# Meta token products over both weight blocks at once, key rows padded to 128, and output transposes moved up in TensorE's order

## The chip, the cores and the metric

The kernel runs on one NeuronCore of a Trainium2 chip. The metric is the device time of one execution in microseconds; the median of three runs before the change is 1068.54 us (1067.28 to 1068.82). The engines named are TensorE (PE, its weight loads PEld), VectorE (DVE), ScalarE (ACT), GpSimd (POOL) and SyncE (SP, which only issues loads).

## The reference, cut to what matters

A decoder block over 1024 tokens of width 1024, with 16 learned meta tokens put in front. Everything starts from one normalised input `h` and a wide product.

```python
z = jnp.concatenate([meta, x], axis=1)                  # 16 + 1024 tokens
h = rms_norm(z, norm_w[l])
p = (h @ w_in[l] + b_in[l]).astype(f32)                 # 1024 x 8192 weights
q, fz, iv, g_hg, u, g_pool, m_hg, m_pool = jnp.split(p, split_at, axis=-1)
log_f = jnp.log(lb + (1.0 - lb) * jax.nn.sigmoid(fz))   # forget gates, 8 heads of 128
k = (1.0 - lb) * jax.nn.sigmoid(-fz)                    # keys
o = hgrn2_chunkwise(q, k, iv, log_f)                    # S = diag(f) S + k v^T, o = S^T q
o = rms_norm(o, hg_norm_w)                              # per head
y_hg = (o * jax.nn.silu(g_hg)) @ w_down_hg[l]
pooled = causal_multiscale_pool(u)                      # windows 2, 4, 8, 16
y_pool = (mixed * pool_scale[l] * jax.nn.silu(g_pool)) @ w_down_pool[l]
merged = jax.nn.sigmoid(m_hg) * y_hg + jax.nn.sigmoid(m_pool) * y_pool
z = z + merged @ w_out[l]
return rms_norm(z, final_norm_w)[:, N_META:]            # meta tokens dropped
```

The meta tokens matter to the output only through what looks back at them: the gates, keys and values of the heads (F and V), and the pooled input (U).

## The kernel before, in words

**Pairs and products.** The weights are cut into blocks of 128 output columns, and two blocks make a pair; there are 40 pairs. `PAIRS` names them: FV (forget gate and value of a head), QG (its query, and the output gate of the head before), and so on; pair 16, in the last turn (j = 8) of the head loop, is an MM pair that has no meta tokens. A pair is computed by a scheme with seven products (`PRODUCTS`) instead of eight, with sums of the four half blocks as weights. Each product has 4 steps of k, and each step 3 matmuls of 128x512: operands are split into a high part (`w_hi`, `r_hi`) and a rest (`w_lo`, `r_lo`), and `three` (line 1149) multiplies high by high, high by rest and rest by high. `half(p, i, part)` issues one half of product i, six matmuls.

**What feeds a product.** For each product ScalarE makes `w_hi` (line 680), VectorE `w_lo` (line 1515), three products ahead of TensorE. ScalarE moves results out of the accumulators (`copy_first`, `last_quarter`), VectorE adds them (`add_11`, ...). All engines run lists written out by hand, and semaphores tie them together; nothing reorders them.

**Meta tokens.** For the 12 pairs FV and U the 16 meta rows are computed apart, in fp32. `meta_product` uses `hm` (the meta tokens, transposed, 16 of 32 columns filled) as stationary operand and the raw weight blocks as moving one: for each block, both halves of k and four column groups of the array, which write to four groups of rows in `acc[3]`. ScalarE copies that to `mt`, and `meta_turn` adds the four groups and turns the result with a small matmul against `stack`; ScalarE places it (`meta_place`). Raw blocks lie in three slots of a ring, block b in slot b % 3.

**A head.** The loop over j = 1 to 8 does the products of pairs FV(j) and QG(j) (14 products, counter n), and puts between them the work of head r = j - 1: `step` (levels of the within-chunk attention, line 1286), `v_transposes`, `k_transposes`, `k_times_v` (for each chunk keys times values; the meta tokens' product is one matmul with 16 rows, line 1305), `outputs` (line 1319, 1320). The normalised output of the head before, `vv`, is turned by `o_transposes(r - 1)` (line 1326), eight transposes, in the middle of product n = 3.

**The way to `o_normed`.** Outputs of head r - 1 are squared on ScalarE (`square_o`); in the next turn VectorE does `ahead(p, 0)`, `mean_o` (line 1768), the operations of `level(r, 0)`, `ahead(p, 1)`, then `normalise_o` (line 1776, two multiplications), which posts `o_normed`; GpSimd takes the power -1/2 in between (line 593). Behind the transposes VectorE's `gated_o` multiplies them with the gate.

Of the kernel before, what the change touches and what calls it, by code (L numbers as in the profile page):

```python
# [6 lines left out]
ACT = mybir.ActivationFunctionType  # L7
AX = mybir.AxisListType
F32 = mybir.dt.float32
# [3 lines left out]
P = 128  # L13
D = 1024
NK = D // P
SEQ = 1024
META = 16
L = META + SEQ
HEADS = 8
CHUNKS = SEQ // P  # L20
LEVELS = 7
STEPS = 6
HALF = 512
KH = NK // 2
# [25 lines left out]
RAWS = 3  # L50
# [62 lines left out]
GROUP = 32  # L113
# [6 lines left out]
def fv(j):  # L120
    return 2 * j

def qg(j):
    return 2 * j + 1
# [30 lines left out]
def hybrid_block(nc, x, meta, norm_w, wstream, pool_w, b_in, lb_logits, hg_norm_w, pool_scale, final_norm_w, out):  # L156
    names = ExitStack()
    with names:
# [4 lines left out]
            "masks_spread", "near_spread", "pool_step", "vec_step", "act_step", "bias_made", "lb_made",  # L163
            "x_squared", "x_mean", "x_rstd", "h_row", "h_tr", "h_hi", "h_copied", "h_lo", "v5_made", "v5_hi",
            "v5_lo", "v6_made", "v6_hi", "v6_lo", "v7_made", "v7_hi", "v7_lo", "v4_made", "v4_hi", "v4_lo",
            "hm_cleared", "hm_copied",
            "sums_made", "w_hi", "w_lo", "wo_hi", "wo_lo", "mm_done", "copied", "added", "c21_done", "meta_mm", "mt_copied", "mt_turned", "meta_placed",
            "qt_made", "prepared", "v_tr", "v_copied", "level_mm", "level_done", "k_tr", "k_copied", "kv_mm",
            "state_done", "o_mm", "o_squared", "o_mean", "o_rstd", "o_normed", "o_tr", "a_made", "a_stored0", "a_stored1",
# [10 lines left out]
        S = {n: names.enter_context(nc.semaphore(n)) for n in sem_names}  # L180
# [4 lines left out]
        def at(name, shape, dtype, offset=None):  # L185
            size = 4 if dtype != U8 else 1
            for n in shape[1:]:
                size *= n
            if offset is None:
                offset = here[0]  # L190
                here[0] += (size + 31) // 32 * 32
            assert offset + size <= 229368, (name, offset + size)
            return nc.alloc_sbuf_tensor_at(name, shape, dtype, offset=offset)
# [24 lines left out]
        w_hi = [at(f"w_hi{n}", [P, KH * P], F32R, ring_at + n * 4096) for n in range(RING)]  # L218
        w_lo = [at(f"w_lo{n}", [P, KH * P], F32R, ring_at + n * 4096 + 2048) for n in range(RING)]
        here[0] = ring_at + RING * 4096  # L220
        raw = [at(f"raw{n}", [P, D], F32) for n in range(RAWS)]
        sums_at = here[0]
        sums = [at(f"sum{n}", [P, HALF], F32) for n in range(4)]
        snaps_at = here[0]
# [6 lines left out]
        hm = at("hm", [P, 2, KH, GROUP], F32)  # L231
# [11 lines left out]
        gt = at("gt", [P, SEQ], F32)  # L243
        gs = at("gs", [P, HALF], F32)
        vv = at("vv", [P, SEQ], F32)
        vm = at("vm", [META, P], F32)
        km = at("km", [META, P], F32)
        st_at = here[0]
        st = at("st", [P, SEQ], F32)
        prod = at("prod", [P, HALF], F32)  # L250
# [5 lines left out]
        mt = at("mt", [P, 2 * P], F32, work + 52736)  # L256
        stack = at("stack", [P, META], F32, work + 53760)
# [65 lines left out]
        acc = [names.enter_context(nc.psum_tensor(f"acc{n}", [P, HALF], F32)) for n in range(4)]  # L323
        levels = names.enter_context(nc.psum_tensor("levels", [P, 2, HALF], F32))
        lev, small = levels[:, 0, :], levels[:, 1, :]
        miscs = names.enter_context(nc.psum_tensor("miscs", [P, 2, HALF], F32))
        misc = (miscs[:, 0, :], miscs[:, 1, :])
        VM, KM, KVM = slice(128, 256), slice(256, 384), slice(384, 512)
# [11 lines left out]
        raw_loaded = (S["raw_loaded0"], S["raw_loaded1"], S["raw_loaded2"])  # L340
# [60 lines left out]
        def turned(p, n):  # L401

            bank = misc[0] if p == 0 else acc[(p + 1) % 2]
            return bank[:, n * META:(n + 1) * META]

        def bias_of(p, n):
            mat, blk = PAIRS[p][1 + n]
# [2 lines left out]
        def raw_half(p, n, half):  # L410
            return raw[(2 * p + n) % RAWS][:, half * HALF:(half + 1) * HALF]
# [8 lines left out]
        def raw_count(p, n):  # L420
            return 16 * ((2 * p + n) // RAWS + 1)
# [115 lines left out]
        def _(pool):  # L537
# [47 lines left out]
            for g in range(GROUPS):  # L585
                rows = slice(g * GROUP, (g + 1) * GROUP)
                pool.tensor_copy(mask[rows, 0, :], whole[rows, rows])
                ins = pool.tensor_copy(mask[rows, 2:MASKS, 0:16], mask1[rows, 2:MASKS, g * 16:(g + 1) * 16])
            ins.then_inc(S["masks_spread"], 1)

            def o_rstd(r):
                pool.wait_ge(S["o_mean"], r + 1)
# [42 lines left out]
            for u in range(16):  # L635
                x = u % 4
                n, t = QUARTERS[x]
# [28 lines left out]
        def _(act):  # L666
# [243 lines left out]

            def copy_v(r):
                act.wait_ge(S["v_tr"], r + 1)
                for q in range(2):
                    act.activation(vv[:, q * HALF:(q + 1) * HALF], misc[q][:, :], ACT.Copy)
                act.activation(vm[:, :], small[0:META, VM], ACT.Copy).then_inc(S["v_copied"], 1)

            def spread_near(r):

# [8 lines left out]
            def copy_k(r):  # L927
                act.wait_ge(S["k_tr"], r + 1)
                for q in range(2):
                    act.activation(ek[:, q * HALF:(q + 1) * HALF], misc[q][:, :], ACT.Copy)  # L930
                act.activation(km[:, :], small[0:META, KM], ACT.Copy).then_inc(S["k_copied"], 1)

            def square_o(r):
                act.wait_ge(S["o_mm"], r + 1)
# [71 lines left out]
            for j in range(1, HEADS + 1):  # L1006
                p, q, r = fv(j), qg(j), j - 1
# [121 lines left out]
            for v in range(2 * CHUNKS):  # L1129
# [3 lines left out]
                if v >= CHUNKS:  # L1133
                    n, t = v - CHUNKS, T_ORDER[v - CHUNKS]
# [9 lines left out]
        def _(pe):  # L1144
# [25 lines left out]
            def meta_turn(p):  # L1170

                pe.wait_ge(S["mt_copied"], META_AT[p] + 1)
                if p:
                    pe.wait_ge(S["c21_done"], p)
                for n in range(2):
                    ins = pe.matmul(turned(p, n), mt[:, n * P:(n + 1) * P], stack[:, :], start=True, stop=True)
                ins.then_inc(S["mt_turned"], 1)

            def meta_product(p):

                if p:
                    pe.wait_ge(S["added"], ADDED[p - 1, 12])
                else:
                    pe.wait_ge(S["hm_copied"], 1)
                for n in range(2):
                    pe.wait_ge(raw_loaded[(2 * p + n) % RAWS], raw_count(p, n))
                    for h in range(2):
                        for k in range(KH):
                            ins = pe.matmul(acc[3][k * GROUP:(k + 1) * GROUP, n * P:(n + 1) * P], hm[:, h, k, :],  # L1190
                                            raw_half(p, n, h)[:, k * P:(k + 1) * P], start=h == 0, stop=h == 1)
                ins.then_inc(S["meta_mm"], 1)

            def half(p, i, part):
# [72 lines left out]
            def step(r, i):  # L1267
                m = STEP_LEVEL[i]
                if m:
                    pe.wait_ge(S["level_done"], r * STEPS + i)  # L1270
                else:
                    pe.wait_ge(S["prepared"], r + 1)
                for c in range(CHUNKS):
                    if m <= 4:
                        for g in range(GROUPS):
                            t = slice(c * P + g * GROUP, c * P + (g + 1) * GROUP)
                            if m == 0:
                                q = ek[:, t]
                            elif m == 1:
                                q = qx[:, :, t].rearrange("p a (b h j) -> p a b h j", h=2, j=2)[:, :, :, 1, :]  # L1280
                            elif m == 2:
                                q = qq[:, c, :].rearrange("p (n t) -> p n t", n=3)[:, :, g * 16:(g + 1) * 16]
                            else:
                                q = qt[:, t.start + 16:t.stop]
                            n = NEAR[m]
                            ins = pe.matmul(lev[g * GROUP:(g + 1) * GROUP, c * n:(c + 1) * n],
                                            kt[:, META + t.start:META + t.stop], q, start=True, stop=True)
                        continue
                    n = 1 << m
                    for h in range(64 // n):  # L1290
                        k0, row = c * P + h * 2 * n, h * 64 + c % 2 * n
                        ins = pe.matmul(lev[row:row + n, c // 2 * n:(c // 2 + 1) * n],
                                        kt[:, META + k0:META + k0 + n], qt[:, k0 + n:k0 + 2 * n], start=True, stop=True)
                ins.then_inc(S["level_mm"], 1)
# [28 lines left out]
            def o_transposes(r):  # L1323
                pe.wait_ge(S["o_normed"], r + 1)
                for c in range(CHUNKS):
                    ins = pe.transpose(misc[c // 4][:, (c % 4) * P:(c % 4 + 1) * P], vv[:, c * P:(c + 1) * P],
                                       ident[:, :])
                ins.then_inc(S["o_tr"], 1)
# [34 lines left out]
            for j in range(1, HEADS + 1):  # L1363
                r = j - 1
                for n in range(2 * PRODUCTS):
                    p, i = fv(j) + n // PRODUCTS, n % PRODUCTS
                    if n == 2:
                        step(r, 1)
                    elif n == 8:
                        step(r, 3)  # L1370
                    elif n == 9:
                        step(r, 4)
                    elif n == 10:
                        step(r, 5)
                    elif n == 11:
                        k_transposes(r)
                    elif n == 12:
                        k_times_v(r)
                    elif n == 13:
                        outputs(r)  # L1380
                    elif n == 5:
                        v_transposes(r)
                    elif n == 6:
                        step(r, 2)
                    half(p, i, 0)
                    if n == 0:
                        step(r, 0)
                    elif n == 3 and r:
                        o_transposes(r - 1)
                    half(p, i, 1)  # L1390

            for p in range(P_POOL, N_PAIRS):
# [8 lines left out]
            for v in range(2 * CHUNKS):  # L1401
                n, t = v // CHUNKS, T_ORDER[v % CHUNKS]
# [894 lines left out]
```

## Time and profile before

| | |
|---|---|
| median of 3 runs | 1068.54 us |
| profiled execution | 1068.12 us |
| its span, first to last instruction | 1066.4 us |
| TensorE matmul, weight load | busy 97%, 79% |
| VectorE, ScalarE, GpSimd | busy 73%, 46%, 9% |
| DMA | mean 98 GB/s |
| mean granted TensorE clock | 0.996 |

The three 128x512 groups of line 1149 alone take 445.7, 434.1 and 433.6 us of busy time, which overlap, since a matmul begins before the one before it is through. For the time that a row costs, the distance to the next row's start is what counts. An fp32 matmul shows as two records. In the profile's timeline an entry of several records runs from the first one's start to the last one's end. A mark in brackets at the end of an entry is the engine's idle time before it and what ended it.

### The profile page before, as it was taken

How to read it: one execution, taken by the hardware profiler on the slowest of the kernel's cores; microseconds unless marked ns; L12 is line 12 of the kernel's file. 1: busy time of each engine (PE TensorE's matmuls, PEld its weight loads, DVE VectorE, ACT ScalarE, POOL GpSimd, SP SyncE). 2: the span in 40 equal slices, each digit the busy share in tenths (PEclk: the TensorE clock that was granted, in tenths of full speed). 3: DMA queues.
4: the chain of work that ended last, by engine and by line, in shares of the span. 5: the costliest groups of instructions: out<-in, count | busy, mean ns of one | idle time of the engine just before them, and what ended most of it. 6: DMA issues, size and time to landing. Idle time of an engine off the chain costs nothing. (4 is left out here: it accounts for less than half of the span.)

```text
span 1066.4 us, 18850 instructions
## 1 busy us (share of the span) xinstructions
PE 1030.7 (97%) x7444; PEld 842.1 (79%) x7444; DVE 781.4 (73%) x1269; ACT 490.0 (46%) x829; POOL 98.0 (9%) x164
## 2 busy tenths in 40 slices
PE   7889999999999999999999999999999999999995
PEld 6668888888888888878888888788887786887884
DVE  7888787878787878787566877864479689878133
ACT  7663535454545453544353433434456345345122
POOL 2500010101010101010101010011100110001111
PEclk9999999999999999999999999999999999999998
DMA  7022020202020202021312222237322764545232
GB/s 261 1 79 80 22 81 21 81 21 81 21 81 21 80 21 80 25 95 53 99 41 89 60 89 79 70 119 266 128 80 98 283 230 158 190 166 178 70 127 100
DMA packets 36055, 104.61 MB, mean 98 GB/s; under 512 B 4576, under 2 KB 4576, under 8 KB 35968
## 3 DMA queue, kind: packets, MB, share of 16 engines
q1 hardware_dynamic: 22064, 65.61, 18.9%
q0 software_dynamic: 8240, 26.79, 6.8%
q10 hardware_dynamic: 5664, 11.02, 2.8%
q8 instruction: 59, 0.97, 0.4%
q14 instruction: 28, 0.23, 0.1%
HBM read 78.23 MB, written 25.17 MB: 97 GB/s over the span
## 5 line engine op out<-in xcount | busy, mean ns | idle before, releaser
L1149 PE MATMUL acc<-r_hi,w_hi 128*128 128x512 f32 x1112 | 445.7, 401 | 14.0 <-DVE w_lo L1515 5.6
L1149 PE MATMUL acc<-r_hi,w_lo 128*128 128x512 f32 x1112 | 434.1, 390 | 0.0
L1149 PE MATMUL acc<-r_lo,w_hi 128*128 128x512 f32 x1112 | 433.6, 390 | 0.0
L1149 PEld LDWEIGHTS acc<-r_hi,w_hi 128*128 128x128 f32 x1112 | 208.8, 188 | 67.0 <-issue 19.9
L1149 PEld LDWEIGHTS acc<-r_hi,w_lo 128*128 128x128 f32 x1112 | 208.7, 188 | 45.1
L1149 PEld LDWEIGHTS acc<-r_lo,w_hi 128*128 128x128 f32 x1112 | 209.1, 188 | 39.7
L680 ACT ACTIVATE w_hi<-sum 128x512 fp32r<-128x512 f32 x156 | 97.8, 628 | 165.6 <-DVE sum L1551 83.4
L1515 DVE TENSOR_TENSOR w_lo<-sum,w_hi 128x512 fp32r<-128x512 f32 x156 | 106.4, 686 | 57.0 <-ACT w_hi L680 56.5
L1515 DVE TENSOR_TENSOR w_lo<-raw,w_hi 128x512 fp32r<-128x512 f32 x120 | 82.1, 687 | 63.5 <-ACT w_hi L680 63.4
L680 ACT ACTIVATE w_hi<-raw 128x512 fp32r<-128x512 f32 x120 | 74.5, 623 | 26.7 <-PE acc L1149 26.7
L1149 PE MATMUL acc<-wo_hi,m_hi 128*128 128x512 f32 x128 | 49.9, 390 | 0.6 <-DVE wo_lo L2188 0.6
L1149 PE MATMUL acc<-wo_lo,m_hi 128*128 128x512 f32 x128 | 49.8, 389 | 0.0
L1149 PE MATMUL acc<-wo_hi,m_lo 128*128 128x512 f32 x128 | 49.8, 389 | 0.0
L764 ACT ACTIVATE second<-acc,bias 128x512 f32<-128x512 f32 x31 | 21.2, 685 | 61.2 <-PE acc L1149 61.0
L593 POOL TENSOR_TENSOR o_rs<-o_ms,minus_half 128x8 f32<-128x8 f32 x8 | 16.0, 2004 | 318.7 <-DVE o_ms L1770 318.7
L764 ACT ACTIVATE first<-acc,bias 128x512 f32<-128x512 f32 x32 | 22.1, 690 | 37.0 <-PE acc L1149 37.0
L764 ACT ACTIVATE fifth<-acc,bias 128x512 f32<-128x512 f32 x31 | 21.3, 687 | 34.5 <-PE acc L1149 34.4
L2052 DVE TENSOR_TENSOR r_lo<-stage,r_hi 128x2048 fp32r<-128x2048 f32 x14 | 32.0, 2285 | 1.9 <-ACT r_hi L1068 1.9
L1149 PEld LDWEIGHTS acc<-wo_hi,m_hi 128*128 128x128 f32 x128 | 24.0, 188 | 6.0 <-DVE wo_lo L2188 1.1
L1149 PEld LDWEIGHTS acc<-wo_hi,m_lo 128*128 128x128 f32 x128 | 24.0, 188 | 5.1
L1149 PEld LDWEIGHTS acc<-wo_lo,m_hi 128*128 128x128 f32 x128 | 24.0, 188 | 5.0
L1553 DVE TENSOR_TENSOR sum<-sum,raw 128x512 f32<-128x512 f32 x38 | 26.3, 692 | 1.3
(287 smaller groups left out, 1369.1 us busy)
## 6 DMA issues: line engine op xcount, KB each, us to landing
raw<-in_wstream SPq DMA_DIRECT2D x88, 512.0 KB, 3.7
xin<-in_x SPq DMA_DIRECT2D x8, 512.0 KB, 6.0
a_spill<-gt POOLq DMA_DIRECT2D x16, 256.0 KB, 3.6
c_spill<-pg POOLq DMA_DIRECT2D x16, 256.0 KB, 2.8
stage<-a_spill ACTq DMA_DIRECT2D x4, 1024.0 KB, 12.2
smh_spill<-zq POOLq DMA_DIRECT2D x16, 256.0 KB, 2.5
gate_in<-smh_spill SPq DMA_DIRECT2D x16, 256.0 KB, 5.2
part_spill<-zq POOLq DMA_DIRECT2D x16, 256.0 KB, 5.5
```

The source lines that it names most:

```text
L593: pool.tensor_tensor(o_rs[:, :], o_ms[:, :], minus_half[:, 0:CHUNKS], ALU.pow).then_inc(S["o_rstd"], 1)
L680: act.activation(w_hi[o % RING][:, :], operand(o), ACT.Copy).then_inc(S["w_hi"], 1)
L764: return act.activation(dst, src, ACT.Identity, bias=b, scale=scale)
L1149: ins = pe.matmul(out_ap, a, b, start=first and n == 0, stop=final and n == 2, skip_group_check=partial)
L1515: dve.tensor_tensor(w_lo[o % RING][:, :], operand(o), w_hi[o % RING][:, :].bitcast(F32), ALU.subtract) \
L1553: dve.tensor_tensor(sums[S4][:, :], sums[S2][:, :], a12, ALU.add).then_inc(done, 1)
L2052: dve.tensor_tensor(r_lo[i][:, :, :], STAGED[i][:, :, :], r_hi[i][:, :, :].bitcast(F32), ALU.subtract) \
```

## The change

Three edits. The meta token products take both weight blocks of a pair as one moving operand of 256 columns: the three raw slots become one tensor, and a slice with a step takes two of them. Where the second block lies in the lower slot, the halves of the result are swapped, and `meta_turn` picks them by `meta_place_of`. The key and value tiles of the meta tokens, `km` and `vm`, get 128 rows instead of 16; GpSimd fills them with zeros once, and ScalarE still writes the first 16. `o_transposes(r - 1)` moves from the middle of product n = 3 to behind `step(r, 1)`, ahead of product n = 2.

```diff
-        raw = [at(f"raw{n}", [P, D], F32) for n in range(RAWS)]
+        raws = at("raws", [P, RAWS, D], F32)
+        raw = [raws[:, n, :] for n in range(RAWS)]
...
-        vm = at("vm", [META, P], F32)
-        km = at("km", [META, P], F32)
+        vm = at("vm", [P, P], F32)
+        km = at("km", [P, P], F32)
...
+        def meta_place_of(p, n):
+
+            return n if 2 * p % RAWS < (2 * p + 1) % RAWS else 1 - n
...
+            pool.wait_ge(S["masks_spread"], 1)
+            pool.wait_ge(S["h_tr"], CHUNKS + 1)
+            pool.memset(vm[:, :], 0.0)
+            pool.memset(km[:, :], 0.0).then_inc(S["meta_cleared"], 1)
...
+                if r == 0:
+                    act.wait_ge(S["meta_cleared"], 1)
...
-                act.activation(vm[:, :], small[0:META, VM], ACT.Copy).then_inc(S["v_copied"], 1)
+                act.activation(vm[0:META, :], small[0:META, VM], ACT.Copy).then_inc(S["v_copied"], 1)
...
-                act.activation(km[:, :], small[0:META, KM], ACT.Copy).then_inc(S["k_copied"], 1)
+                act.activation(km[0:META, :], small[0:META, KM], ACT.Copy).then_inc(S["k_copied"], 1)
...
-                    ins = pe.matmul(turned(p, n), mt[:, n * P:(n + 1) * P], stack[:, :], start=True, stop=True)
+                    place = meta_place_of(p, n)
+                    ins = pe.matmul(turned(p, n), mt[:, place * P:(place + 1) * P], stack[:, :], start=True, stop=True)
...
+                slots = [(2 * p + n) % RAWS for n in range(2)]
                 for n in range(2):
-                    pe.wait_ge(raw_loaded[(2 * p + n) % RAWS], raw_count(p, n))
-                    for h in range(2):
-                        for k in range(KH):
-                            ins = pe.matmul(acc[3][k * GROUP:(k + 1) * GROUP, n * P:(n + 1) * P], hm[:, h, k, :],
-                                            raw_half(p, n, h)[:, k * P:(k + 1) * P], start=h == 0, stop=h == 1)
+                    pe.wait_ge(raw_loaded[slots[n]], raw_count(p, n))
+                both = raws[:, min(slots):max(slots) + 1:max(slots) - min(slots), :]
+                for h in range(2):
+                    for k in range(KH):
+                        ins = pe.matmul(acc[3][k * GROUP:(k + 1) * GROUP, 0:2 * P], hm[:, h, k, :],
+                                        both[:, :, h * HALF + k * P:h * HALF + (k + 1) * P], start=h == 0, stop=h == 1)
...
                     if n == 2:
                         step(r, 1)
+                        if r:
+                            o_transposes(r - 1)
...
-                    elif n == 3 and r:
-                        o_transposes(r - 1)
```

TensorE's queue in the turn j = 2 before the change, from the level-0 group to the middle of product 3 (out<-operands, then the shape of the output and how many stand in a row; 61, 62 are the operands of products 2 and 3):

```order
L1286 MATMUL levels<-ek,kt 32x32 x32
L1190 MATMUL acc<-raw_91,hm 32x128 x8
L1190 MATMUL acc<-raw_89,hm 32x128 x8
...
L1286 MATMUL levels<-qx,kt 32x32 x32
L1176 MATMUL acc<-stack,mt 128x16 x2
L1149 MATMUL acc<-r_hi_61,w_hi_83 128x512
...
L1149 MATMUL acc<-r_hi_62,w_lo_88 128x512
L1326 MATMUL miscs<-ident,vv 128x128 x8
L1149 MATMUL acc<-r_hi_62,w_hi_84 128x512
```

The same stretch after the change:

```order
L1302 MATMUL levels<-ek,kt 32x32 x32
L1206 MATMUL acc<-raws,hm 32x256 x8
...
L1302 MATMUL levels<-qx,kt 32x32 x32
L1342 MATMUL miscs<-ident,vv 128x128 x8
L1190 MATMUL acc<-stack,mt 128x16 x2
L1162 MATMUL acc<-r_hi_61,w_hi_83 128x512
...
L1162 MATMUL acc<-r_hi_62,w_lo_88 128x512
L1162 MATMUL acc<-r_hi_62,w_hi_84 128x512
```

Sixteen meta matmuls became eight with twice the columns, and the eight transposes stand 18 product matmuls and the turning of the meta products earlier. The lists of VectorE, ScalarE and SyncE hold the same work in the same order; GpSimd's has the two fills behind its masks.

## Rows read from the trace of the kernel before

**Rows 1.** Page, part 1: busy us (share of the span) xinstructions.
```profile
PE 1030.7 (97%) x7444; PEld 842.1 (79%) x7444; DVE 781.4 (73%) x1269; ACT 490.0 (46%) x829; POOL 98.0 (9%) x164
```
**Rows 2.** Waits on TensorE, longest in total first: us in total, times, longest.
```profile
PE acc L1149 <- DVE w_lo L1515: 5.6, 5, 1.8
```
**Rows 3.** Timeline of TensorE, turn j = 2: start us, us, engine, instruction, count.
```profile
139.64 0.76 PE L1286 MATMUL levels<-qx,kt 128*32 128x32 f32 x64
140.33 0.62 PE L1176 MATMUL acc<-stack,mt 128*128 128x16 f32 x4
...
145.02 1.04 PE L1326 MATMUL miscs<-ident,vv 128*128 128x128 f32 x8
```
**Rows 4.** Timeline of VectorE, turn j = 2, up to the multiplications.
```profile
135.34 0.69 DVE L1515 TENSOR_TENSOR w_lo<-sum,w_hi 128x512 fp32r<-128x512 f32 x1 [2.93 <-ACT w_hi L680]
135.95 1.22 DVE L1768 TENSOR_REDUCE o_ss<-vv 128x8 f32<-128x1024 f32 x1
...
140.05 1.28 DVE L1776 TENSOR_TENSOR vv<-miscs,o_rs 128x512 f32<-128x512 f32 x2
```
**Rows 5.** Timeline of all engines, turn j = 8.
```profile
461.09 0.68 DVE L1690 TENSOR_TENSOR qx<-qx,fg 128x512 f32<-128x512 f32 x1
...
461.82 0.76 PE L1286 MATMUL levels<-qx,kt 128*32 128x32 f32 x64 [0.78 <-DVE qx L1690]
462.30 1.27 DVE L1776 TENSOR_TENSOR vv<-miscs,o_rs 128x512 f32<-128x512 f32 x2
```
**Rows 6.** Timeline of all engines in the early stage, at the longest wait.
```profile
52.12 0.69 DVE L1515 TENSOR_TENSOR w_lo<-sum_early,w_hi 128x512 fp32r<-128x512 f32 x1 [1.64 <-ACT w_hi L680]
...
52.96 0.47 PE L1149 MATMUL levels<-r_hi,w_hi 128*128 128x512 f32 x1 [2.38 <-DVE w_lo L1515]
```
**Rows 7.** Timeline of GpSimd, turn j = 2.
```profile
137.45 2.06 POOL L593 TENSOR_TENSOR o_rs<-o_ms,minus_half 128x8 f32<-128x8 f32 x1 [53.76 <-DVE o_ms L1770]
```
**Rows 8.** Timeline of ScalarE, turns j = 1 and 2.
```profile
98.44 0.25 ACT L915 ACTIVATE vm<-levels 16x128 f32<-16x128 f32 x1
...
133.54 0.67 ACT L764 ACTIVATE gt<-acc,bias 128x512 f32<-128x512 f32 x1
...
134.68 0.62 ACT L680 ACTIVATE w_hi<-sum 128x512 fp32r<-128x512 f32 x1
```
**Rows 9.** Timeline of TensorE, turn j = 1, at keys times values.
```profile
120.71 0.39 PE L1149 MATMUL acc<-r_hi,w_lo 128*128 128x512 f32 x1
121.03 0.48 PE L1305 MATMUL levels<-vm,km 16*128 16x128 f32 x2
121.44 1.83 PE L1308 MATMUL miscs<-vv,ek 128*128 128x128 f32 x14
123.02 0.48 PE L1149 MATMUL acc<-r_hi,w_hi 128*128 128x512 f32 x1
```
**Rows 10.** Timeline of TensorE, turn j = 1, at the outputs.
```profile
125.61 0.40 PE L1149 MATMUL acc<-r_hi,w_lo 128*128 128x512 f32 x1
125.85 0.39 PE L1319 MATMUL miscs<-st,qx 128*128 128x128 f32 x2
...
129.20 0.39 PE L1320 MATMUL miscs<-vv,att 128*128 128x128 f32 x2
129.34 0.47 PE L1149 MATMUL acc<-r_hi,w_hi 128*128 128x512 f32 x1
```
**Rows 11.** Timeline of GpSimd behind the masks.
```profile
79.81 0.62 POOL L609 DMA_DIRECT2D smp_spill<-st  x1 [36.38 <-ACT st L821]
```
**Rows 12.** Timeline of TensorE, turn j = 2, at the meta products.
```profile
134.32 1.08 PE L1190 MATMUL acc<-raw,hm 128*32 128x128 f32 x32
```
**Rows 13.** Stretches: length, busy us (records) of each engine, PEclk, DMA share, GB/s.
```profile
40.00:44.00 4.00, 2.97 (x12) 2.17 (x12) 3.23 (x6) 2.97 (x3) 3.25 (x9) 1.00 0.02 4
...
50.50:53.00 2.50, 0.12 (x2) 0.07 (x1) 0.88 (x2) 2.49 (x4) 0.00 (x0) 1.00 0.00 0
53.00:57.00 4.00, 4.00 (x11) 3.17 (x12) 4.00 (x6) 0.13 (x1) 0.00 (x0) 0.57 0.00 0
```

More of the change, by code:

```diff
@@ L165, in hybrid_block @@
             "v5_lo", "v6_made", "v6_hi", "v6_lo", "v7_made", "v7_hi", "v7_lo", "v4_made", "v4_hi", "v4_lo",
-            "hm_cleared", "hm_copied",
+            "hm_cleared", "meta_cleared", "hm_copied",
             "sums_made", "w_hi", "w_lo", "wo_hi", "wo_lo", "mm_done", "copied", "added", "c21_done", "meta_mm", "mt_copied", "mt_turned", "meta_placed",
```

## The prediction
> **What bounds the kernel now.** I read the busy shares first: TensorE's matmul row is busy for 97% of the span [rows 1]. The view of waits on TensorE then tells how much of the rest could be regained. Its longest line is 5.6 us in five waits, against 1066.4 us of span [rows 2]. The kernel is one queue of TensorE instructions, so a microsecond taken from the queue is a microsecond gained, and so is one added as a wait. The third view is the order of time around the three places that the change touches, in the attention loop (head j = 2 stands for all), on TensorE and on the engines that feed it.
>
> **Part 1, the output transposes: a new wait.** Seven heads (r - 1 = 0 to 6) move their eight transposes from the middle of product 3 to the place right behind the 64 level-1 records, ahead of product 2; the eighth keeps its place in the stage behind the loop. The transposes need `o_normed`, which VectorE posts behind the second of its two multiplications on line 1776.
> When does TensorE come to the new place? The level-1 records start at 139.64, and the next work, the turning of the meta token products, starts at 140.33 [rows 3]. So TensorE is free for the transposes at 140.33.
> When is `o_normed` there? The multiplications start at 140.05 and last 1.28, so they end at 141.33 [rows 4]. From a VectorE end to the start of a TensorE instruction that has waited for it I have two measures: 461.09 + 0.68 = 461.77 to 461.82, that is 0.05 [rows 5], and 52.12 + 0.69 = 52.81 to 52.96, that is 0.15 [rows 6]. I take 0.10 between them. The transposes then start at 141.43 and TensorE has stood for 1.10 us. In the last of the seven heads the level-1 records start at 461.82, are done after the same 0.69 at 462.51, and the multiplications end at 462.30 + 1.27 = 463.57 [rows 5]: 463.67 - 462.51 = 1.16. Seven waits at 1.11 are 7.8 us; with 0.05 and 0.15 as the ends, 7.4 to 8.2.
> In the old place this cost nothing: the transposes started at 145.02 [rows 3], 3.7 us behind the end of the multiplications. That is the cover which the move takes away.
> Does the wait come once, or in every head? It depends on what starts VectorE's run up to line 1776. At 135.34 VectorE has stood 2.93 us for ScalarE's `w_hi`; from there on it works without an idle mark: weight remainder, sum of squares, level 0, weight remainder, multiplications, 5.99 us in all [rows 4]. GpSimd's power in between is done at 137.45 + 2.06 = 139.51, before it is wanted [rows 7]. ScalarE's `w_hi` at 134.68 stands right behind two operations that read the last product of the pair before, the first at 133.54 [rows 8], and those wait for TensorE. So the whole run hangs on TensorE's end of the previous pair. If TensorE is late, VectorE is as late, and the next head waits again. The last head shows the same lock from the other side: there is no meta product in that pair, TensorE comes early and already waits 0.78 us for VectorE's level 0 [rows 5].
> Behind TensorE's waiting transposes stand the turning of the meta products, product 2 and all that follows; who waits for those is ScalarE and VectorE, which both have idle time. VectorE doesn't get its work done sooner, since it waits for TensorE's products again a few instructions on.
> The transposes themselves cost the same at both places within a few hundredths. At the new place the shape of the stationary tile already changes there from 128*32 to 128*128 [rows 3], so no second change comes. I count -0.03 for a handover saved, an estimate from the starts that lie 0.24 behind a product record against 0.223 between equal neighbours [rows 10]: -0.2 for seven, with 0 to -0.7 as ends.
>
> **Part 2, keys and values of the meta tokens padded to 128 rows: a gain.** Before, the product of 16 rows starts at 121.03, that is 0.32 behind the last product record at 120.71; the next, full-size matmuls start only 0.41 later, and the following product at 123.02 [rows 9]. From 120.71 to 123.02 are 2.31 us for eight fp32 matmuls, of two records each. What full-size neighbours take stands in the outputs of the same head: first start 0.24 behind the last product record (125.61, 125.85), then fifteen steps to 129.20, which is 3.35 / 15 = 0.223 each, then 0.14 to the product [rows 10]. Eight of them: 0.24 + 7 x 0.223 + 0.14 = 1.94. The gain is 2.31 - 1.94 = 0.37, in eight heads 3.0 us. The ends are 0 (the 16 rows are not the reason of the gaps) and 3.1.
> The tiling page of the Trainium skill argues against such padding: TensorEngine Tiling (Array Packing), section When to Use Tiling, recommends row tiling for a contraction of up to 64 rows. If the padded matmul cost what tiling is said to gain, the 3.0 us would be lost and the sum come to rival (b). Here there is one such matmul in a head and nothing to stand beside it, and the rows show two slow handovers around it; the trace decides for the gain.
> The padding needs zeros: two fills of 128x128 on GpSimd, once. They stand behind the masks, where GpSimd has been idle for 36.38 us before its next operation [rows 11], and `vm` isn't written by ScalarE before 98.44 [rows 8]. Nothing at the end of GpSimd's queue moves. If their use of the memory disturbs VectorE in that busy stretch, it is by less than a microsecond: 0, with ends -0.5 and +0.7.
>
> **Part 3, meta token products over 256 columns: nothing.** Twelve pairs have 16 fp32 matmuls (32 records) with 128 moving columns, and would have 8 (16 records) with 256. And whatever is gained in the six pairs of heads j = 2 to 7 lies between the end of the pair before and the new wait; the wait swallows it, since `o_normed` doesn't come earlier. Six pairs count (heads 0 and 1, four pooling pairs). Ends: +0.2 (the doubled row costs 0.04 more) and -2.4 (see the rival). I take 0.
>
> **Sum.** +7.8 - 0.2 - 3.0 + 0 = +4.6 us. The profiled execution took 1068.12 us (span 1066.4), the median of the runs is 1068.54, 0.4 above it. 1068.5 + 4.6 = 1073.1 us, 0.43% slower.
>
> **Rivals.**
> (a) The wait comes once. If VectorE's run up to the multiplications had a pace of its own, TensorE would be late by 1.1 us in its first head and meet `o_normed` without a wait from then on: 1068.5 + 1.1 - 3.0 - 0.2 = 1066.4, faster by 0.2%. It decides from a wait of under 0.46 us a head on average (3.2 / 7). For it: VectorE is busy for 6 us without a pause. Against it: the 2.93 us of idle time at the head of these. 7 in 100.
> (b) The padding gains nothing: 1068.5 + 7.8 - 0.2 = 1076.1. For it: no trace here shows this product at 128 rows. Against it: its neighbours, the same in all else, have no such gaps. 6 in 100.
> (c) The number of records, not of columns, sets the pace of the meta products. Half the records would save half of 0.81, 0.40 us, in six pairs 2.4: 1070.7. Against it: the level-1 group has 64 records in the 0.69 us from 139.64 to 140.33 [rows 3], 11 ns each, so 26 ns is no floor of records. 5 in 100.
> The same tiling page, section Instruction Overhead, gives some 60 cycles for every matmul; by that, 16 records fewer would be an estimated 16 x 60 / 2.4 GHz = 0.4 us a pair, as in this rival. The 11 ns a record speak against it where four stand side by side.
> (d) The new wait lowers TensorE's clock. After TensorE was busy for 0.12 of 2.50 us the granted clock of the next 4 us was 0.57, that is mostly 1.2 GHz, a loss of 1.7 us; after a stretch with 2.97 of 4.00 busy it stayed at 1.00, 2.4 GHz [rows 13]. A pause of 1.1 us is nearer to the second. With a fall in each head: 1073.1 + 7 x 1.7 = 1085. 3 in 100.
>
> **How the numbers follow.** My forecast has 76 in 100, its own range is 1071.7 to 1074.4 (7.4 to 8.2 for the waits, 2.5 to 3.1 for the padding, 0.7 for the early stage). The remaining 3 in 100 are for a shift in the first 80 us, where TensorE still waits for VectorE and any shift may help or harm by 2 us. The range reaches down to between (a) and (c) and up to (b): 1069.6 to 1076.4. About 0.2%, 2.1 us, can be told from no change here. Slower by more: the forecast, (b), (d), a part of (c), 0.87; within: a part of (a) and (c) and the rest, 0.07; faster: half of (a) and some of the rest, 0.06.
>
> **What would show it.** Right: in the waits on TensorE a new line, transposes for VectorE's `vv`, seven times, some 7.8 us together, each at 1.05 to 1.25; the meta key product in full size, 0.22 us before its neighbour; 0.24 instead of 0.32 before it; the meta product group still near 1.0 us; heads 2 to 7 longer by 0.7 us each. Wrong: such a line with one wait (a), gaps that stay around the meta key product (b), a meta group of 0.6 us (c), a granted clock under 1.00 in the loop (d).

## The result, and the profile after

| | before | after |
|---|---|---|
| median | 1068.24 us (8 runs) | 1071.29 us (8 runs, 1070.37 to 1073.91) |
| ratio to before, 95% interval | | 1.0029 (1.0017 to 1.0040) |
| profiled execution | 1068.12 us | 1070.37 us |
| its span | 1066.4 us | 1068.6 us |

The change makes the kernel slower by 3.1 us, between 1.8 and 4.3. The forecast was 1073.1, that is 4.6 slower than the 1068.54 that it started from; the median of eight runs before is 0.3 lower than that.

The waits on TensorE after (us in total, times, longest us; the first two lines) have a new line at their head, ahead of the one that led before [rows 2]:

```profile
PE miscs L1342 <- DVE vv L1792: 6.9, 7, 1.0
PE acc L1162 <- DVE w_lo L1531: 5.6, 5, 1.7
```

It is the output transposes for VectorE's normalised output, seven times. TensorE's timeline in the turn j = 2 (start us, us, instruction, count, idle before) shows one of them; it answers to [rows 3]:

```profile
138.68 0.76 PE L1302 MATMUL levels<-qx,kt 128*32 128x32 f32 x64
140.44 1.09 PE L1342 MATMUL miscs<-ident,vv 128*128 128x128 f32 x8 [1.00 <-DVE vv L1792]
141.37 0.52 PE L1190 MATMUL acc<-stack,mt 128*128 128x16 f32 x4
141.74 0.47 PE L1162 MATMUL acc<-r_hi,w_hi 128*128 128x512 f32 x1
```

By the prediction's way of counting TensorE could have begun 0.69 behind the start of the levels, at 139.37, and began at 140.44: it stood for 1.07 us. In the seven turns it is 1.03 to 1.11, together 7.45. The view of waits counts from the end of the last level record, 0.07 later, and so has 6.9. VectorE's timeline of the same turn says for what; it answers to [rows 4]:

```profile
134.40 0.69 DVE L1531 TENSOR_TENSOR w_lo<-sum,w_hi 128x512 fp32r<-128x512 f32 x1 [2.93 <-ACT w_hi L691]
...
138.51 0.68 DVE L1531 TENSOR_TENSOR w_lo<-sum,w_hi 128x512 fp32r<-128x512 f32 x1
139.11 1.27 DVE L1792 TENSOR_TENSOR vv<-miscs,o_rs 128x512 f32<-128x512 f32 x2
```

The run from 134.40 to 140.38 is 5.98 us long, as it was (5.99), without a pause, and it still begins behind 2.93 us of idle time for ScalarE's `w_hi`. From 140.38 to TensorE's start are 0.06.

The meta key product is in full size and has lost its gaps; TensorE's timeline, turn j = 1, to be read beside [rows 9]:

```profile
120.16 0.39 PE L1162 MATMUL acc<-r_hi,w_lo 128*128 128x512 f32 x1
120.39 0.38 PE L1321 MATMUL levels<-vm,km 128*128 128x128 f32 x2
120.61 1.73 PE L1324 MATMUL miscs<-vv,ek 128*128 128x128 f32 x14
122.09 0.48 PE L1162 MATMUL acc<-r_hi,w_hi 128*128 128x512 f32 x1
```

From product record to product record are 1.93 us instead of 2.31. The meta token products have half the records and the same length. In turn j = 2 the first product behind them was, before (to be read with [rows 12]),

```profile
135.33 0.50 PE L1149 MATMUL acc<-r_hi,w_hi 128*128 128x512 f32 x1
```

and after, with the group itself:

```profile
133.37 1.07 PE L1206 MATMUL acc<-raws,hm 128*32 128x256 f32 x16
134.37 0.50 PE L1162 MATMUL acc<-r_hi,w_hi 128*128 128x512 f32 x1
```

1.00 us from their start to the product's; before it was 135.33 - 134.32 = 1.01.

A turn of the head loop as a whole is the distance between two meta key products. From the second to the third:

```profile
174.77 0.48 PE L1305 MATMUL levels<-vm,km 16*128 16x128 f32 x2
...
228.44 0.48 PE L1305 MATMUL levels<-vm,km 16*128 16x128 f32 x2
```

before, and after:

```profile
174.63 0.38 PE L1321 MATMUL levels<-vm,km 128*128 128x128 f32 x2
...
228.91 0.38 PE L1321 MATMUL levels<-vm,km 128*128 128x128 f32 x2
```

53.67 against 54.28, 0.61 us more a turn. The granted clock of the loop is untouched; the same stretch before and after, with length, busy us of PE, PEld, DVE, ACT and POOL, clock, DMA share and GB/s:

```profile
130.00:510.00 380.00, 378.68 (x4059) 309.56 (x4058) 296.29 (x578) 181.66 (x325) 25.08 (x26) 1.00 0.17 53
```

```profile
130.00:510.00 380.00, 371.78 (x3946) 304.53 (x3945) 295.75 (x575) 178.84 (x320) 25.05 (x26) 1.00 0.16 53
```

TensorE's busy time in these 380 us falls by 6.9, as much as the new line of waits adds up to.

### The profile page after: what moved, and what is told of

Its sections match the earlier page's. It is cut to its first block and busy times, and to the rows that moved or that the text cites. A ratio compares the mean times of both kernels' runs of the same rounds, so it can differ in the third digit from the quotient of the medians.

```text
span 1068.6 us, 18470 instructions
## 1 busy us (share of the span) xinstructions
PE 1026.7 (96%) x7252; PEld 837.3 (78%) x7252; DVE 781.6 (73%) x1269; ACT 490.1 (46%) x829; POOL 98.1 (9%) x166
## 5 line engine op out<-in xcount | busy, mean ns | idle before, releaser
L1531 DVE TENSOR_TENSOR w_lo<-raws,w_hi 128x512 fp32r<-128x512 f32 x120 | 82.0, 686 | 63.8 <-ACT w_hi L691 63.0
L691 ACT ACTIVATE w_hi<-raws 128x512 fp32r<-128x512 f32 x120 | 74.5, 623 | 27.1 <-PE acc L1162 27.1
L1569 DVE TENSOR_TENSOR sum<-sum,raws 128x512 f32<-128x512 f32 x38 | 26.3, 692 | 1.3
```

The costliest lines, as they stand in the source:

```text
L691: act.activation(w_hi[o % RING][:, :], operand(o), ACT.Copy).then_inc(S["w_hi"], 1)
L1531: dve.tensor_tensor(w_lo[o % RING][:, :], operand(o), w_hi[o % RING][:, :].bitcast(F32), ALU.subtract) \
L1569: dve.tensor_tensor(sums[S4][:, :], sums[S2][:, :], a12, ALU.add).then_inc(done, 1)
```

## The experiments

The loop's turns are compared by the distance of the meta key products in each profile; "mean turn" is the distance of the first to the eighth, over 7. It was 53.67 before and is 54.21 after. The ratio of an experiment is to the kernel before, run again beside it: 1067.70 us for experiments 1 to 4, 1067.92 for 5 to 8.

**1. No move.** The changed kernel, with the transposes back at their old place:

```diff
                     if n == 2:
                         step(r, 1)
-                        if r:
-                            o_transposes(r - 1)
...
+                    elif n == 3 and r:
+                        o_transposes(r - 1)
```

> Padding and 256-column meta products as in the changed kernel, the transposes back in the middle of product 3. My theory (a repeated wait at the new place costs, the padding gains 0.38 us a head): no wait of the transposes, 3.1 us faster than before, about 1065.1, ratio 0.997. Rival (the wait comes once, rival a): 1067 or more is left to the other edits, so the ratio would be 0.999 or above. Rival (the padding gains nothing): 1068.2.

Measured: 1064.96 us, ratio 0.9970 (0.9959 to 0.9980). No wait of the transposes is left, the mean turn is 53.30. Against the changed kernel's 54.21 the move costs 0.91 us a turn, 6.4 us in seven.

**2. The move only.** The kernel before, with the transposes moved:

```diff
                     if n == 2:
                         step(r, 1)
+                        if r:
+                            o_transposes(r - 1)
...
-                    elif n == 3 and r:
-                        o_transposes(r - 1)
```

> The kernel before with the transposes moved and nothing else. My theory: seven waits of some 1.0 us, less 0.15 us a head that the handovers at the new place save, so 6.5 us slower than before, about 1074.7, ratio 1.006. Rival (the wait comes once): at most 1.1 us slower, 1069.3. The later handovers at the level steps unchanged.

Measured: 1075.1 us, ratio 1.0073 (1.0060 to 1.0085). It is 7.4 us slower than before (6.4 to 9.1 by the interval), where 6.5 was expected. Its waits begin with

```profile
PE miscs L1326 <- DVE vv L1776: 6.9, 7, 1.0
```

and its mean turn is 54.61, 0.94 more than before: 6.6 us in seven. Rival (a), one wait at the start of the loop, would have left the other six turns as they were; it has fallen.

**3. The padding only.** The kernel before, with tiles of 128 rows and the two fills (the three raw slots are one tensor here too, which changes no instruction's work):

```diff
-        vm = at("vm", [META, P], F32)
-        km = at("km", [META, P], F32)
+        vm = at("vm", [P, P], F32)
+        km = at("km", [P, P], F32)
...
+            pool.memset(vm[:, :], 0.0)
+            pool.memset(km[:, :], 0.0).then_inc(S["meta_cleared"], 1)
```

> The kernel before with the 128-row tiles and nothing else. My theory: 8 x 0.38 = 3.1 us faster, 1065.1, and the key product 0.11 us a record as its neighbours. Rival (the gaps around the key product are not from its 16 rows): no gain, 1068.2.

Measured: 1064.98 us, ratio 0.9972 (0.9961 to 0.9983), at the expected place, and the mean turn is 53.31. Rival (b) has fallen.

**4. The 256-column meta products only.** The kernel before with the loop over both weight blocks replaced by the one matmul of 256 columns, with the tensor and the choice of halves that it needs:

```diff
-                for n in range(2):
...
-                            ins = pe.matmul(acc[3][k * GROUP:(k + 1) * GROUP, n * P:(n + 1) * P], hm[:, h, k, :],
-                                            raw_half(p, n, h)[:, k * P:(k + 1) * P], start=h == 0, stop=h == 1)
+                        ins = pe.matmul(acc[3][k * GROUP:(k + 1) * GROUP, 0:2 * P], hm[:, h, k, :],
+                                        both[:, :, h * HALF + k * P:h * HALF + (k + 1) * P], start=h == 0, stop=h == 1)
```

> The kernel before with the 256-column meta products and nothing else. My theory (columns set the pace): 0.01 us a pair, 0.1 us in all, 1068.1, ratio 1.000. Rival (records set the pace, rival c): 0.4 us a pair in twelve pairs, 4.8 us faster, 1063.4.

Measured: 1068.13 us, ratio 1.0004 (0.9995 to 1.0012). The mean turn is 53.66, and the group takes as long as before, in TensorE's timeline:

```profile
135.06 1.07 PE L1200 MATMUL acc<-raws,hm 128*32 128x256 f32 x16
136.06 0.50 PE L1156 MATMUL acc<-r_hi,w_hi 128*128 128x512 f32 x1
```

Rival (c), a pace set by the number of records, is out: it would be 1063.4.

The medians of experiments 2, 3 and 4 add up to 7.4 - 2.7 + 0.4 = +5.1 us, the change as a whole has +3.1. Each of the four is known to about 1 us either way, so the gap of 2.0 is within what they can tell; the turns, at 6.6 and -2.5 for move and padding, with the eighth key product's -0.4, add up to +3.7.

**5. The multiplications one place earlier.** The changed kernel, with one swap in VectorE's list:

```diff
-                ahead(p, 1)
                 if r:
                     normalise_o(r - 1)
+                ahead(p, 1)
```

> The changed kernel, with one swap in VectorE's list: the two multiplications that make the normalised output stand ahead of the weight remainder before them (0.6 us). My theory (TensorE's wait is VectorE's run, seven times): the multiplications start when GpSimd's power is done, 0.5 us earlier, each wait falls from 1.0 to 0.5, 7 x 0.5 = 3.5 us faster than the changed kernel, about 1067.8. Rival (the wait is something else than VectorE's order): 1071.3 as without the swap.

Measured: 1068.81 us, ratio to before 1.0008 (0.9999 to 1.0016), where the changed kernel has 1.0029. It gives back 2.2 us by the ratios and 2.8 by the turns (mean turn 53.81), not the 3.5 that were expected. The waits shrink to

```profile
PE miscs L1342 <- DVE vv L1792: 4.1, 7, 0.6
```

The reason is in the timelines of GpSimd and VectorE (one after the other):

```profile
137.83 2.06 POOL L604 TENSOR_TENSOR o_rs<-o_ms,minus_half 128x8 f32<-128x8 f32 x1 [53.36 <-DVE o_ms L1786]
```

```profile
139.22 0.68 DVE L1706 TENSOR_TENSOR qx<-qx,fg 128x512 f32<-128x512 f32 x1
139.99 1.29 DVE L1792 TENSOR_TENSOR vv<-miscs,o_rs 128x512 f32<-128x512 f32 x2
```

GpSimd's power is done at 139.89, and the multiplications start at 139.99. Elsewhere in this run an operation of VectorE starts some 0.60 behind one of 0.68 (in the changed kernel 138.51 to 139.11), which would be 139.82; so the power now ends last and takes 0.17 of the 0.6. They begin 4.27 behind the start of VectorE's run (135.72), where in the changed kernel it was 4.71: 0.44 earlier, and the mean wait fell from 0.99 to 0.59. This edit touches nothing on TensorE, and it moves TensorE's wait by 0.40, nearly as much as it moves VectorE's work: the wait is VectorE's run.

**6. The transposes in the middle of product 2.** As experiment 1, but six product matmuls behind the place of the change:

```diff
-                    elif n == 3 and r:
+                    elif n == 2 and r:
                         o_transposes(r - 1)
```

> The changed kernel, with the transposes in the middle of product 2, six product matmuls (1.4 us) later than in the change. My theory (only the wait counts, not the place): the wait is gone, the time is that of the place in product 3, about 1065.1. Rival (an early place costs by itself, through handovers of the array): above 1066.

Measured: 1064.32 us, ratio 0.9966 (0.9954 to 0.9978), no wait of the transposes, mean turn 53.29. It can't be told from experiment 1. What counts is on which side of `o_normed` the transposes stand.

**7. Padding to 64 rows.** As experiment 3, with fewer rows. One run, so that the distances in its profile count and not its time.

```diff
-        vm = at("vm", [P, P], F32)
-        km = at("km", [P, P], F32)
+        vm = at("vm", [64, P], F32)
+        km = at("km", [64, P], F32)
```

> The kernel before with key and value tiles of 64 rows (zeros in rows 16 to 63). Theory A (any matmul on fewer than 128 rows makes TensorE empty itself before and after): gaps stay, 0.32 ahead and 0.2 between records, 2.31 us from product to product. Theory B (only a small tile of 32 rows does): 1.93 us, as with 128 rows.

Measured: 1069.23 us in one run. TensorE's timeline, turn j = 1:

```profile
121.32 0.39 PE L1162 MATMUL acc<-r_hi,w_lo 128*128 128x512 f32 x1
121.64 0.48 PE L1319 MATMUL levels<-vm,km 64*128 64x128 f32 x2
122.06 1.83 PE L1322 MATMUL miscs<-vv,ek 128*128 128x128 f32 x14
123.64 0.47 PE L1162 MATMUL acc<-r_hi,w_hi 128*128 128x512 f32 x1
```

0.32 ahead of the product and 2.32 from product record to product record: the gaps are those of 16 rows. The mean turn is 53.71, as before (53.67). What theory A says of the gaps holds: padding to 64 rows gains nothing, and padding to the neighbours' 128 does. That TensorE empties itself in them is not seen in a row.

**8. The move in one turn.** The changed kernel, with the transposes at the new place for r = 4 alone and in the middle of product 3 for the others:

```diff
-                        if r:
+                        if r == 4:
                             o_transposes(r - 1)
...
+                    elif n == 3 and r and r != 4:
+                        o_transposes(r - 1)
```

> The changed kernel with the transposes moved in one turn alone (r = 4), the others in product 3. My theory (a wait is not given back): one wait of 1.0 us, TensorE 0.9 us later from there to the end of the loop than with no move. Rival (later turns take it up): the distance goes back to 0 within a turn or two.

Measured: 1064.98 us in one run, and one wait:

```profile
PE miscs L1342 <- DVE vv L1794: 1.0, 1, 1.0
```

Its meta key products from the third on start at

```profile
227.39 0.38 PE L1321 MATMUL levels<-vm,km 128*128 128x128 f32 x2
...
280.67 0.38 PE L1321 MATMUL levels<-vm,km 128*128 128x128 f32 x2
...
334.96 0.38 PE L1321 MATMUL levels<-vm,km 128*128 128x128 f32 x2
...
388.29 0.38 PE L1321 MATMUL levels<-vm,km 128*128 128x128 f32 x2
```

The turns between them are 53.28, 54.29 and 53.33. The turn with the wait is 1.0 longer than its neighbours (0.93 longer than the same turn of experiment 1, 53.36), and the next one has its old length: the wait isn't given back.

It also shows what VectorE does. Its run up to the multiplications begins, in the turn with the wait and in the two behind it, at

```profile
294.69 0.69 DVE L1533 TENSOR_TENSOR w_lo<-sum,w_hi 128x512 fp32r<-128x512 f32 x1 [2.93 <-ACT w_hi L691]
...
348.99 0.69 DVE L1533 TENSOR_TENSOR w_lo<-sum,w_hi 128x512 fp32r<-128x512 f32 x1 [2.93 <-ACT w_hi L691]
...
402.32 0.69 DVE L1533 TENSOR_TENSOR w_lo<-sum,w_hi 128x512 fp32r<-128x512 f32 x1 [2.94 <-ACT w_hi L691]
```

54.30 and 53.33: behind the turn in which TensorE stood, VectorE starts 1.0 us later, as TensorE does. A run with a pace of its own would have started at its old distance. This is why the wait is there again in each turn of the changed kernel.

## Why the prediction was right, and where it was off

**The sign and the mechanism** were right. The chain was: TensorE reaches the new place before `o_normed`, VectorE's run is as late as TensorE is, so the wait recurs in each turn. The seven waits stand in the profile, experiments 1 and 2 put the cost on the move by removing it and by doing it alone, experiment 5 changes the wait through VectorE's list alone, and experiment 8 shows one late turn of TensorE making VectorE's next run as late. Through which instruction is less certain than the prediction has it. It names ScalarE's operation at 133.54, which reads the last product of the pair before. No idle time stands ahead of that one: ScalarE had worked without a pause since 132.44, behind 1.06 us of idle time that ended with VectorE's `qx`. So the lateness may come through VectorE's own earlier work, which also waits for products, and no run separates the two ways.

**The size of the stand** was nearly right: 1.11 us a head forecast, 1.07 from 139.37 to 140.44, and 7.45 in seven where 7.8 were forecast. The sign that was named for it, a line of waits of 7.8 us with each at 1.05 to 1.25, came as 6.9 us with none above 1.03, since that view begins to count 0.07 later than the sum did. The measured 0.06 from VectorE's end to TensorE's start is at the lower of my two measures [rows 5, 6].

**The padding** was right: 0.37 a head forecast, 2.31 - 1.93 = 0.38 measured, 3.1 us in eight. Beside full-size neighbours the product starts 0.23 behind the last product and its neighbour 0.22 behind it, as was said.

**The meta products** were right: 0.01 us a pair, and nothing in the runs. Rival (c) priced 16 records a pair; an fp32 matmul is two records, so it is eight matmuls fewer. Neither count shows in the time.

**The step that was mis-sized** is the term for the handovers, "-0.03 for a handover saved" and -0.2 in all. The net cost of the move in a turn is 0.91 to 0.94, and the stand alone is 1.06 on average, so the new place gives back 0.12 to 0.15 a turn, some 1.0 us in seven, and not 0.2. It can be counted out in turn j = 2. From the start of the turning of the meta products (140.33 [rows 3]) thirty product matmuls follow, with the transposes among them, to

```profile
148.45 0.39 PE L1149 MATMUL acc<-r_hi,w_lo 128*128 128x512 f32 x1
```

that is 8.12 us. After the change the thirtieth is

```profile
148.40 0.39 PE L1162 MATMUL acc<-r_hi,w_lo 128*128 128x512 f32 x1
```

at 148.40 - 141.37 = 7.03, and the transposes ahead took 141.37 - 140.44 = 0.93, together 7.96. The difference is 0.16. At the old place the transposes stood between

```profile
144.78 0.40 PE L1149 MATMUL acc<-r_hi,w_lo 128*128 128x512 f32 x1
...
145.81 0.49 PE L1149 MATMUL acc<-r_hi,w_hi 128*128 128x512 f32 x1
```

and the next product matmul started at 146.13. Less two steps of 0.227 that is 1.35 - 0.45 = 0.90 for them. At the new place they take 0.93, and the turning of the meta products behind them takes 0.10 less than before (0.37 against 0.47), so 0.83. Handovers thus give 0.07 a turn where 0.03 were forecast, and the other 0.09 is the pace of the product matmuls, which the prediction had put at nothing: small matmuls slow the products behind them a little, and the move leaves one such place where there were two. The last section has that pace, and how much of the 0.09 is scatter.

**The sum.** With the measured terms the loop comes to +6.4 (7 x 0.91) - 3.1 = +3.3 us; the loops of the two profiles agree: from the first meta key product to the eighth TensorE takes 7 x (54.21 - 53.67) = 3.8 us longer, and the gain at the eighth itself, 0.38, comes behind that, which leaves +3.4. The medians give +3.1. The spans of the two profiles differ by 2.2 only, because the one before comes 0.6 us later to its first meta key product and takes 0.6 us longer behind the loop, that gain left out. The forecast of +4.6 took the handovers 0.9 us too small, the stands 0.3 us too large and the padding 0.1 us too small, and its own range (1071.7 to 1074.4) just missed 1071.29, while the wide one (1069.6 to 1076.4) held it. Another 0.3 us of the distance is the start at 1068.54 instead of 1068.24. The own range doesn't come out of the terms that are named for it (they give 1071.9 to 1074.7), and it leaves out the 0 to -0.7 for the handovers, the very term that was off. Heads were to be 0.7 us longer; they are 0.54.

**Rival (d)** didn't come: the granted clock of the loop is 1.00 in spite of seven stands of 1.07 us.

**Not settled:** behind the loop the profiled executions differ by up to 1.3 us, the gain of the eighth key product left out. In the stage of the down projections TensorE waits for VectorE's `zq`, in some once for 0.5 or 0.6 us and in others twice for 0.9 to 1.4 together. Both are seen with and without the move, and what decides it wasn't tried.

**A better version.** Padding without the wait is faster than both kernels: 1064.96 (experiment 1), 1064.98 (3) and 1064.32 (6), whose intervals overlap.

## What to carry to other kernels

Before moving an instruction forward in a bound engine's queue, read from the trace when its operand is ready, not only whether the place is convenient: here the old place had 3.7 us of cover and the new one lacked 1.1. If the producer's run starts later whenever the bound engine is late, the wait recurs in every turn; a producer with a pace of its own would make it come once, but no run here has such a one. A matmul on few rows between full-size ones can cost more than a full-size one, and then filling its rows with zeros pays: 0.38 us each at the neighbours' 128 rows, nothing at 64.

## What the runs showed of the hardware that was not expected

**The pace of product matmuls after a burst of small ones.** Behind the transposes the 128x512 matmuls can start 232 ns apart instead of 227. TensorE's timeline before the change, turn j = 2:

```profile
146.13 0.40 PE L1149 MATMUL acc<-r_lo,w_hi 128*128 128x512 f32 x1
...
148.22 0.39 PE L1149 MATMUL acc<-r_lo,w_hi 128*128 128x512 f32 x1
```

nine steps in 2.09, 232 ns each. After it, behind the stand of the same turn:

```profile
142.28 0.39 PE L1162 MATMUL acc<-r_hi,w_lo 128*128 128x512 f32 x1
...
144.32 0.39 PE L1162 MATMUL acc<-r_hi,w_lo 128*128 128x512 f32 x1
```

nine steps in 2.04, 227 ns. This turn is an exception, though. Three turns later, in the same profile and behind an equal stand, it is

```profile
305.11 0.40 PE L1162 MATMUL acc<-r_hi,w_lo 128*128 128x512 f32 x1
...
307.18 0.39 PE L1162 MATMUL acc<-r_hi,w_lo 128*128 128x512 f32 x1
```

2.07, 230 ns. Over nine steps from the second product matmul on, the seven turns of the changed kernel have 227 to 231 ns behind the stand, those of experiment 2 have 229 to 231. Before the change it was 231 in all six turns behind `meta_turn`, and 228 to 232 behind the transposes. So the stand is no cure for the slower pace: some 0.04 us is lost behind most bursts, and of the two that the move touches it leaves one. In experiment 1, with the transposes at the old place, the thirty product matmuls of turn j = 2 take 8.07 us and not 8.12, so up to 0.05 of the 0.16 belongs to the execution.

The four small matmuls of `meta_turn` are faster behind the transposes in every turn: 141.37 to 141.74, 0.37, against 0.47 from 140.33 to 140.80 before, behind the level steps. Experiment 5 gives back 0.14 a turn with a stand of 0.65 us, so what is given back doesn't grow with the stand. Why small matmuls slow what follows them, no run tested.

**Tiles of 64 rows** among tiles of 128 cost the same gaps as tiles of 16 (experiment 7). The Trainium skill says so: in TensorEngine Tiling (Array Packing), section Tiling Modes, a change of the tiling mode drains TensorE, and 64 rows are a mode of their own there. The trace agrees as far as the gaps go, with 0.32 us ahead of the key product at 64 rows instead of 0.23 at 128.

**The clock in the first 30 us** differs from execution to execution. In the profile of experiment 1, TensorE's clock fell for 3.4 us early on, which it didn't in the profiles before and after; the same stretch of experiment 1 and of before:

```profile
23.50:27.00 3.50, 3.50 (x10) 2.60 (x9) 2.77 (x6) 1.82 (x5) 1.74 (x2) 0.51 0.00 0
```

```profile
23.50:27.00 3.50, 3.50 (x19) 2.93 (x20) 3.06 (x6) 2.70 (x6) 0.93 (x1) 1.00 0.00 0
```

0.51 is the lower level, 1.2 GHz, nearly throughout, and 10 records of matmuls instead of 19 began in it. TensorE had been busy to much the same extent in the 14.5 us ahead of it (10.43 and 10.38 us). It costs 1.6 us: from the first product matmul of this stretch (22.61 in experiment 1, 23.49 before) to the one behind the longest early wait (53.66 and 52.96, [rows 6]) it is 31.05 instead of 29.47. It fell so in four of the ten profiled executions (experiments 1, 4, 5 and 7), with different kernels. The changed kernel and experiments 1, 5, 6 and 8 are the same program up to there, and it fell in two of these five; so it belongs to the execution and not to the edits. The four are those in which that first product matmul started earliest, at 22.55 to 22.68, against 22.78 to 23.49 in the other six. A kernel's runs scatter over some 3 us, and 1.6 of that can be this. That is why the lengths of turns above say more on a single edit than the spans do.
